# Expert rows by a slot-to-token table and gathers instead of a scatter and loads (one core, Trainium2)

## The reference, cut to what matters

```
h = rmsnorm(x)                                  # 640 x 1024
lg = h @ w_rg + b_rg                            # top 1 of 4 groups
le = h @ w_re + b_re                            # then top 2 of that group's 4 experts
for e in range(16):
    y = (silu(h @ w_eg[e]) * (h @ w_eu[e])) @ w_ed[e]
    out = out + gate[..., e:e+1] * y
x = x + out
x = x + sigmoid(rmsnorm(x) @ w_ple_gate) * (p @ w_ple_proj)
```

## Time and profile before

| what | us |
|---|---|
| median of 3 runs (1021.66 to 1024.14) | 1023.14 |
| the profiled execution | 1026.18 |
| its span on the core | 1024.5 |
| TensorE busy in the span | 916.8 |
| VectorE / ScalarE / GpSimd busy | 575.0 / 537.5 / 126.8 |
| DMA queue of SP: bytes moved | 170.84 MB |
| DMA queue of POOL: bytes moved | 30.09 MB |

### The profile page before, as it was taken

How to read it: one execution, slowest core, us unless ns; L and a number is a source line. 1 busy time by engine, 2 the same in 40 slices (tenths; PEclk the granted TensorE clock), 3 DMA queues, 4 the chain that set the end, 5 groups by cost and what they waited for, 6 DMA issues and landing times.

```text
span 1024.5 us, 14705 instructions
## 1 busy us (share of the span) xinstructions
PE 916.8 (89%) x5119; PEld 772.0 (75%) x5119; DVE 575.0 (56%) x775; ACT 537.5 (52%) x732; POOL 126.8 (12%) x225
## 2 busy tenths in 40 slices
PE   5999999979999899899999963899999999993698
PEld 4788999745588778789987853688888777772586
DVE  4566236423234434433343551799999889894852
ACT  5302321589566646622232241688888788783431
POOL 3455600122200000000000012000000000002500
PEclk9999999989999999999999986999999999997699
DMA  8025891000256445263320068899999999997411
GB/s 290 12 83 159 252 280 42 2 0 1 71 179 182 120 137 184 88 202 88 111 90 4 7 240 341 311 354 394 391 394 392 391 392 392 393 390 266 140 52 51
DMA packets 121786, 201.49 MB, mean 197 GB/s; under 512 B 6686, under 2 KB 44222, under 8 KB 121744
## 3 DMA queue, kind: packets, MB, share of 16 engines
q1 hardware_dynamic: 113104, 170.84, 48.0%
q0 software_dynamic: 8640, 30.09, 8.6%
HBM read 173.60 MB, written 27.30 MB: 196 GB/s over the span
## 4 chain that ended last, share of the span: by engine, by line
PE 63%; DVE 9%; DMA 8%; ACT 7%; SPq 6%; issue 6%; POOL 2%; DVEq 0%; ACTq 0%; POOLq 0%
PE bank L432 18%; PE bank L433 17%; PE bank L434 17%; SPq L378 5%; DMA raw<-in_w_exp_down 5%; DVE wlo L402 2%; PE bank L1777 2%; PE bank L1667 2%; PE bank L1843 1%; PE bank L1807 1%; DVE sums L1356 1%; DMA x<-in_x_prompt 1%; POOL moe_rows L748 1%; ACT whi L398 1%; PE bank L1820 1%
## 5 line engine op out<-in xcount | busy, mean ns | idle before, releaser
L402 DVE TENSOR_TENSOR wlo<-raw,whi 128x1024 fp32r<-128x1024 f32 (+1 forms) x266 | 312.2, 1190 | 149.5 <-ACT whi L398 139.3
L398 ACT ACTIVATE whi<-raw 128x1024 fp32r<-128x1024 f32 (+1 forms) x266 | 272.6, 1033 | 172.4 <-PE bank L434 137.8
L432 PE MATMUL bank<-hh,whi 128*128 128x320 f32 x448 | 142.7, 319 | 1.4 <-DVE al L1146 1.4
L433 PE MATMUL bank<-hh,wlo 128*128 128x320 f32 x448 | 140.7, 314 | 0.0
L434 PE MATMUL bank<-hl,whi 128*128 128x320 f32 x448 | 140.2, 313 | 0.0
L432 PE MATMUL bank<-whi,hh 128*128 128x512 f32 x280 | 113.8, 406 | 9.3 <-DVE hl L1146 7.0
L432 PE MATMUL bank<-whi,xh 128*128 128x512 f32 x256 | 103.9, 406 | 9.7 <-DVE xl L1146 5.6
L434 PE MATMUL bank<-wlo,hh 128*128 128x512 f32 x280 | 111.0, 396 | 0.0
L433 PE MATMUL bank<-whi,hl 128*128 128x512 f32 x280 | 110.9, 396 | 0.0
L434 PE MATMUL bank<-wlo,xh 128*128 128x512 f32 x256 | 101.3, 396 | 0.0
L433 PE MATMUL bank<-whi,xl 128*128 128x512 f32 x256 | 101.2, 395 | 0.0
(11 more groups left out here) (261 smaller groups left out, 1412.3 us busy)
## 6 DMA issues: line engine op xcount, KB each, us to landing
raw<-in_w_exp_gate SPq DMA_DIRECT2D x64, 512.0 KB, 11.2
raw<-in_w_exp_up SPq DMA_DIRECT2D x64, 512.0 KB, 11.7
raw<-in_w_exp_down SPq DMA_DIRECT2D x64, 512.0 KB, 12.4
raw<-in_w_in SPq DMA_DIRECT2D x40, 512.0 KB, 6.4
moe_rows<-zero POOLq DMA_DIRECT2D x16, 512.0 KB, 13.1
kc<-in_cache_k SPq DMA_DIRECT2D x16, 512.0 KB, 3.6
vc<-in_cache_v SPq DMA_DIRECT2D x8, 1024.0 KB, 5.3
xe<-moe_rows SPq DMA_DIRECT2D x16, 512.0 KB, 10.8
```

What stands on the lines that cost most here:

```text
L398: nc.scalar.activation(part(whi[:, u.slot], short), part(raws[u.raw], short), ACT.Copy).then_inc(s_hi, 1)
L402: nc.vector.tensor_tensor(out=part(wlo[:, u.slot], short), in0=part(raws[u.raw], short), in1=part(whi[:, u.slot], short).bitcast(F32), op= ...
L432: pe.matmul(out, a_hi, b_hi, start=first, stop=False, skip_group_check=True)
L433: pe.matmul(out, a_lo, b_hi, start=False, stop=False, skip_group_check=True)
```

## The change

- The zero fill of the 16 x 128 rows is gone. The scatter stays only in the overflow branch.
- SP stores each tile of `h2` to a DRAM tensor `normed_rows` (`h2d`) as soon as it is normed, ahead of the load of `lnb` and of expert 0's weights.
- A table says for each slot which token it holds. DVE makes `ids` (token numbers by choice: the row within the tile, and 128 times the tile) and `spot` (one 1 where a token's rank equals the column), TensorE multiplies them (20 products of 128 x 16, summed in one bank), DVE copies the sum to `table`. An empty slot holds 0, that is token 0. The ranks are read from the bank without the copy `rk`.
- The rows of each expert come by an indirect transfer on POOL from `normed_rows` with a column of `table`. The first two wait for the stored rows and the table alone, and stand ahead of the flag. The gather for expert e, from 2 on, waits for the transposes of e - 2; the stores of `y` follow three experts behind. SP loads no rows any more and waits for no scatter.
- `xh` and `xl` exist twice; the rows of expert 1 are transposed and split between the gate and the up product of expert 0.
- The overflow sum moves from the second to the fourth tile of the second `w_ple_proj` unit, and the flag with it.

```
+            for t in range(NT):
+                sp.wait_ge(s_hn, NT + t + 1)
+                sp.dma_start(h2d[t * P:(t + 1) * P, :], h2[:, t]).then_inc(s_h2, 16)
...
-            sp.wait_ge(s_scat, 16 * 2 * NT)
-            for e in range(2):
-                sp.dma_start(xe[:, e], Xd[e * C:(e + 1) * C, :]).then_inc(s_xe[e], 16)
...
+            def expert_rows(e):
+                if e >= 2:
+                    pool.wait_ge(s_xt, 2 * e - 2)
+                pool.indirect_dma_start(out=xe[:, e % 2, :], out_offset=None, in_=h2d[:, :],
+                                        in_offset=bass.IndirectOffsetOnAxis(ap=table[:, e:e + 1], axis=0)
+                                        ).then_inc(s_xe[e % 2], 16)
+
+            pool.wait_ge(s_h2, 16 * NT)
+            pool.wait_ge(s_table, 1)
+            expert_rows(0)
+            expert_rows(1)
             pool.wait_ge(s_flag, 1)
...
+            for e in range(2, NE):
+                expert_rows(e)
+                if e >= 3:
+                    store_y(e - 3)
+            for e in range(NE - 3, NE):
+                store_y(e)
...
+            ve.tensor_scalar(ids[:, 0], Mk[:], pid[:, 0:1], None, ALU.mult).then_inc(s_ids, 1)
+            for t in range(NT):
+                ve.tensor_scalar(ids[:, 1, :, t], Mk[:, :, t], float(P * t), None, ALU.mult).then_inc(s_ids, 1)
...
+            tt(spot[:].rearrange("p k t c -> p (k t) c"), iota[:, None, :].to_broadcast([P, 2 * NT, P]),
+               slotf[:, 0].rearrange("p k t -> p (k t)")[:, :, None].to_broadcast([P, 2 * NT, P]), ALU.is_equal
+               ).then_inc(s_place, 1)
+            dve.wait_ge(s_tab, 1)
+            ve.tensor_copy(table[:], bank[6][:, 2 * P:2 * P + NE]).then_inc(s_table, 1)
...
                 if t == 1:
+                    pe.wait_ge(s_place, 1)
+                    pe.wait_ge(s_ids, 1 + NT)
+                    out = bank[6][:, 2 * P:2 * P + NE]
+                    for k in range(2):
+                        for s in range(NT):
+                            for n in range(2):
+                                ins = pe.matmul(out, spot[:, k, s], ids[:, n, k, s], start=k + s + n == 0,
+                                                stop=k == 1 and s == NT - 1 and n == 1, skip_group_check=True)
+                    ins.then_inc(s_tab, 1)
+                if t == 3:
                     pe.wait_ge(s_ovm, 1)
...
             expert_rows(0, 0, 0)
-            gate_or_up(Unit(U_M), 0, 0)
-            gate_or_up(Unit(U_M + 4), 0, 1)
+            gate_or_up(Unit(U_M), 0, 0, 0)
             expert_rows(1, 1, 0)
+            gate_or_up(Unit(U_M + 4), 0, 0, 1)
```

More of the change, by code:

```diff
@@ L183, in program @@
         Mb = sb("Mb", [P, NT, NE], BF16)
-        rk = sb("rk", [P, NT, NE])
+        iota = sb("iota", [P, P])
+        pid = sb("pid", [P, 1])
+        table = sb("table", [P, NE], I32)
         mr = sb("mr", [P, 2, NT, NE])
@@ L262, in program @@
         bank = [ctx.enter_context(nc.psum_tensor(f"bank{i}", [P, 512], F32)) for i in range(8)]
+        h2d = nc.dram_tensor("normed_rows", (T, D), F32, kind="Internal").ap()
         Xd = nc.dram_tensor("moe_rows", ((NE * C) + NE * OV_TILES * P, D), F32, kind="Internal").ap()
@@ L743, in _, with store_y @@
                                    zero[:, None, :].to_broadcast([P, D // P, P])).then_inc(s_zero, 16)
[L744 to L751, removed]
-                pool.wait_ge(s_y, 2 * e + 2)
[L753 to L757, removed]
+                pool.wait_ge(s_zero, 16 * NE * OV_TILES)
+                for t in range(NT):
+                    for k in range(2):
+                        pool.indirect_dma_start(out=Xd[:, :], out_offset=bass.IndirectOffsetOnAxis(
+                            ap=slot[:, k, t:t + 1], axis=0), in_=h2[:, t, :], in_offset=None).then_inc(s_scat, 16)
+                pool.wait_ge(s_scat, 16 * 2 * NT)
+            def store_y(e):
+                pool.wait_ge(s_y, 2 * e + 2)
+                pool.dma_start(Yd[e * C:(e + 1) * C, :], y[:, e % 2]).then_inc(s_yo[e % 2], 16)
+            for e in range(2, NE):
[4 more added lines that the diff above has]
+                store_y(e)
             with pool.If(over > 0):
@@ L1570, in hidden_lo @@
                    ALU.subtract).then_inc(s_htl, 1)
-            rows_lo(0)
-            for j in range(4, 11):
+            rows_lo(0, 0)
+            for j in range(4, 8):
+                lo(U_M + j)
+            rows_lo(1, 1)
+            for j in range(8, 11):
                 lo(U_M + j)
@@ L2006, in product, with gate_or_up @@
                 ins.then_inc(s_mm, 5)
-            def gate_or_up(u, e, which):
+            def gate_or_up(u, e, par, which):
                 if which == 0:
@@ L2014, in gate_or_up @@
                 for i in range(4):
-                    product(u.plus(i), bank[which][:, :], xh, xl, 2 * i, i == 0, i == 3)
+                    product(u.plus(i), bank[which][:, :], xh[:, par], xl[:, par], 2 * i, i == 0, i == 3)
             def hidden_rows(e):
```

72 lines of the change are left out of this document (38 added, 34 removed).

## The result

The changed kernel takes 1007.63 us (median of four runs, 1004.79 to 1009.34), beside 1023.42 for the kernel before: a ratio of 0.9845, 95% interval 0.9818 to 0.9873, or 15.8 us less. The forecast was 20 less. Its profiled execution took 1009.34 us, with a span of 1007.6.

A forecast was written before the change was run, and what follows sets the result against it. The prediction took the expert weight stream on the DMA as the bound: 10.4 + 2.5 + 7.0 = 19.9 us, taken as 20, gives 1006 against the profiled execution and 1003.0 against the median; range 997 to 1011.

The forecast's parts named there:

- dear gathers: Rival, chance 0.04: repeated or scattered rows make each of 14 gathers occupy the DMA x us longer; 1031 at x = 2.
- no effect: Rival, chance 0.03: something else on POOL's queue or the stores hold the first gather until about 622; 1021 to 1023 us.
- The sum that places the end of before: Expert stage before the change: 626.6 + 286.2 for 214 transfers + 2.5 first landing + 8.2 unused capacity = 923.5 us.
- The chain to the table: Router to first gather: DVE makes `ids`, ranks and `spot` (608.6), TensorE multiplies (609.7), table copied by 609.9, `xe` 0 lands 615.7.
- The end of the `pp` copies: Hand-over to experts: last `pp` copy 6.4 us behind the table products, at 616.1, with first transposes set at 616.2.
- The stream's start: Hand-over on SP: expert 1's weight loads go out at 616.2 instead of 626.6, 10.4 us earlier.
- The two `xe` loads: Hand-over: the first two `xe` transfers, 2 x 1.337 = 2.7 us, are nearly done by the stream's start; 2.5 taken.
- Unused capacity: DMA capacity left unused early in the expert stage, 8.2 us before; without TensorE's stall buffers come free, 7.0 us back.
- no window far below 390: Sign of being right: between 620 and 900 us no window's DMA rate is far below 390 GB/s.
- the pause stays: Rival, chance 0.18: expert 0's weight splits still hold buffers back, the 7 us are not recovered; gain 13, time 1010 us.
- TensorE's front: TensorE from hand-over to expert 1: 12.9 earlier transposes + 3.5 first-gate clock + 4.0 wait + 1.6 later clock = 22.0 us.
- The two fronts: After the hand-over: TensorE's work gains 22.0 us, the weight stream 19.9; the stream moves less and sets the end.

The follow-up runs named there:

- the clock kept: The changed kernel with idle TensorE products added: 26 ahead of the ranks, 4 ahead of the table, 36 small ones ahead of the first gate; 1003.6 us, ratio 0.9804.
- store later: The changed kernel with the fifth `h2` store and the load of `lnb` moved behind expert 0's first four weight units; 1003.0 us, ratio 0.9791.
- gathers twice: The changed kernel with each of the 14 gathers for experts 2 to 15 done a second time into unused rows; 1024.03 us, ratio 1.0012.
- spread: The changed kernel with empty slots naming 128 different tokens instead of all naming token 0; 1006.61 us, ratio 0.9826.

## Why the prediction was right or wrong

- **What bounds, and the sign: right.** Two runs show it from both sides: 10.7 us of delay in the stream cost 10.4, and 18.7 us taken from it gave 7.4 (5.2 up to the stage's last product) and then bound on TensorE. The rivals "dear gathers" and "no effect" fell: 1.2 to 1.35 us per gather, and the first gather goes out 0.85 us behind the table's copy. Taking out the zero fill gave nothing that the rows show, as forecast: the last norm starts at 584.86 instead of 584.20.
- **The sum that places the end of before** is less exact than it looks. It counts the two first loads of `xe` among its 16 and again as 2.5 us until 629.1, in which the DMA moved 325 GB/s and left 0.4 us unused; with 0.4 in place of 2.5 it gives 921.4, not 923.5. The row at 921.52 isn't the last split either: two more follow from 922.96. The changes forecast don't depend on it.
- **The chain to the table: right, within about 1 us.** `spot` was put at 1.5 us and took 1.49; the twenty products end at 609.28 (forecast 609.7), the table is there at 609.5 (609.9), the first gather starts at 610.34 (610.5). Counted from the last norm, which came 0.66 us later than in before, all of these are about 1 us earlier than forecast. The `h2` store in front was put at 1.7: expert 0's first split moved from 9.38 us behind the last norm's square (593.58 - 584.20) to 11.20 (596.06 - 584.86), 1.8, but the router's chain, which waits for the second split as well, only from 13.59 (597.79) to 14.79 (599.65), 1.2.
- **The end of the `pp` copies: a term that was put too low.** I took 6.4 us behind the table products from the kernel before. There the wait for the ranks was followed by one tile at the slow level of the clock, and the four tiles behind it ran at the fast one. Here the table's wait comes after the first tile, and the same four tiles took 8.44 us, at 0.77. The copies ended at 617.74 instead of 616.1, and expert 1's weights with them. Keeping TensorE at work there and ahead of the first gate gave the 6.5 us back, 3.6 us in the stage and 4.2 in the whole run (with overlapping intervals). The duration was right for its clock; I had not asked whether the clock would be the same.
- **The stream's start**: 10.4 forecast; counted from the last norm, 9.5 (8.8 from the start of the span, since that norm came 0.66 later). The two `xe` loads: 2.5 forecast, 2.7 in the sum (2 x 1.337); no run parts them from the rest.
- **Unused capacity**: 7.0 of 8.2 forecast, 5.7 of 8.6 came. The pause at 650 is gone, and the order of the rows of expert 1 is its cause: putting it back brought the hole back and cost 4.4 of the 15.8 us. Part of what remains goes with the same slow clock, the first gate at 0.72 and the DMA at 347 GB/s: with the clock kept 1.7 instead of 2.9 us stay unused. So the sign "no window far below 390" was missed. The rival "the pause stays" fell by these rows; the time alone, 1007.6, lies nearer to its 1010 than to 1003.
- **TensorE's front**: 12.9 + 3.5 + 4.0 + 1.6 forecast. The 3.5 for the first gate's clock did not come: behind 0.69 and 2.31 us of waiting the first gate ran at the slow level, as before. The first hidden rows moved by 16.4 us (657.97 to 641.57), not 22. This cost little by itself, as TensorE's front has about 5 us to spare, but the slow first gate goes with part of the unused capacity above.
- **The two fronts are not independent**, and my sum treated them so. Sending weights earlier without moving TensorE was worth nothing (24.2 us instead of 32.9, but 11.1 unused instead of 2.9); moving the chain ahead of TensorE moved both.
- **Together**: 9.5 + 2.7 + 5.7 = 17.9 against a forecast of 19.9; the stage did end 17.9 earlier. Ahead of the stage 0.66 is lost and behind it 0.33, neither forecast, so the profiled executions differ by 16.84 (1026.18 - 1009.34); the medians by 15.8, since the profiled execution of after lies less far above its median (1.7 us) than that of before (2.8). The time came out inside the range, 4.6 us above the forecast: some 2 us of this are terms of the sum, the rest lies outside the stage and in which execution was profiled.

## What to carry to other kernels

Before you take a duration of TensorE from a row, look at the clock of that stretch and ask whether a new wait in front of it will change it: here 26 products took 6.5 us or 8.44. Where a stream of loads and the engine that frees its buffers both start at a hand-over, move the chain that both wait for (here DVE's order and one store), not the issue of the loads. Here a gather by a table costs the stream no more than a load of the same bytes, even when many places name one row, so it can replace a scatter through DRAM where the table is early.

## What the runs showed of the hardware

- A gather of 128 rows takes POOL 0.94 us while DVE stands idle (the result gathers at 925.57 and 926.82). In the expert stage, where DVE is busy for 17.0 of 18 us, the twelve gathers from 656.84 on took 1.86 us seven times, 3.40 twice and 0.96 to 1.13 three times; the stores of `y` from the same queue stay at 0.53 to 0.59. This is the rule the prediction named (the Trainium skill, SBUF — State Buffer, "SBUF: two separate sides"), and the rows agree with it for the operation that reads an index list: the gather at 656.84 began during a DVE subtraction (656.63) and took 1.86, the one at 630.75 began just ahead of one (630.79) and took 0.94. No run was made to show that this lock is the cause. TensorE never waits for `xe` in after, so it costs nothing here.
- Waits on TensorE were followed by the slow level of the clock (1.2 GHz) twice around the hand-over in after: behind 6.71 us (the ranks), and again, at 0.72, behind waits of 0.69 and 2.31 us with the transposes between them. In "store later" the same two waits ahead of the first gate were followed by a first product of 0.50 us and a clock of 1.00 from 618 to 630, so the wait alone does not decide; what does is not settled here. The last down product, behind 2.6 to 3.6 us of waiting, ran at 1.00, 0.77 or 0.64 from run to run.
- Where the stream sets the end it holds 391 to 393 GB/s in the window from 800 to 880, and 392 to 393 over the 200 us from 700 to 900 in before and with gathers twice or spread.
